# Neighbourhood attention's scores from split operands; the convolution's end and PE's waits rearranged

## The chip, the cores and the metric

One core of one Trainium2 chip. The metric is the device time of one execution in microseconds. The core has the engines PE (matmuls), DVE (elementwise and reductions), ACT (activations, copies), POOL (GpSimd) and SP (here it only issues DMAs). Each works through its own queue in order; semaphores tie the queues together.

## What is computed

A block of 256 rows of width 2048 (feed-forward, attention, feed-forward), then two hybrid layers on it and on a context of 256 rows, all in fp32. What matters here is the mixer of a hybrid layer:

```python
def mix_out(p, na_out, ...):
    ya = multiscale_pool(p[..., OFF_A_V:OFF_A_G], ...) * silu(p[..., OFF_A_G:OFF_B_Q])
    yb = na_out * silu(p[..., OFF_B_G:OFF_C_U])
    yc = conformer_conv(p[..., OFF_C_U:OFF_C_G], ...) * silu(p[..., OFF_C_G:PROJ_WIDTH])
    return concatenate([ya, yb, yc]) @ w_out

# neighbourhood attention, 16 heads of 64 columns: q, k turned by axial_rope,
# scores of local keys (with bias rpb, masked) and of the context's keys, one softmax over both
s_loc = einsum(q * 64**-0.5, k) + bias;  s_ctx = einsum(q * 64**-0.5, kc)
p = softmax(concatenate([s_loc, s_ctx]));  out = p_loc @ v + p_ctx @ vc

def conformer_conv(u, conv_dw, conv_dw_b, ln_g, ln_b, conv_pw, conv_pw_b):
    y = u[..., :512] * sigmoid(u[..., 512:])
    y = depthwise_conv(y, conv_dw, 31 taps) + conv_dw_b
    yn = layer_norm(y) * ln_g + ln_b
    return silu(yn) @ conv_pw + conv_pw_b
```

In the first hybrid layer the context's rows go through all of it too (their queries see the context's keys only); in the second they give keys and values only.

## The kernel before

**The ring.** All weights stream from HBM through one ring: SP loads 512 KB units, ACT copies each 512-column piece to `hi` as fp32r (L392), DVE makes `lo` = raw - hi (L396), and PE takes three single-pass fp32r products for each piece and row tile, in `mm3`: hi by hi (L401), lo by hi (L402), hi by lo (L403). The three together stand in for an fp32 product. Before a projection the activations are turned and split in the same way (`hT`, `uT`).

**A hybrid layer** (`ly` 0 and 1, with `nt` = 4 and 2 row tiles) is: norm and modulation (`z_turn`, `rows_over`, in which PE spreads the row norms with a product of `ones` and `sdg`); five chunks of w_in, ca0 or ca1, with pooling and gated convolution input beside them; the chunks q, k, v, g of w_in, whose results go to `qkvg`, while DVE runs the 31 taps of the convolution (L1578), 128 steps on `cv`, which a memset clears first; then the convolution's end; then the neighbourhood section; then w_out.

**The convolution's end.** DVE adds the bias to `cv` (L1589, semaphore cf_b). PE waits for that, for cpw and cpb (cf_in: two DMAs that SP can issue only when the ring's last piece is used) and for all copies out of the banks, and turns `cv` into four banks (L2128). DVE takes the statistics, ACT the root; then for each tile t: DVE `zb` (L1609), PE turns it (`normed_turn`, L2137), ACT makes `sT` (L960), PE multiplies by cpw in fp32 (`pointwise`, L2147 and L2148), DVE multiplies by the gate (`conv_gate`, L1604). PE's order is turn(t + 1), pointwise(t). ACT makes Silu of the attention's gates behind all this (L967). GpSimd adds the mask to the bias table `ball` in eight instructions, as soon as that table has landed (L2329).

**The neighbourhood section** runs eight pairs of heads, one to a lap (`na_laps`). A unit is one head and one row tile; the two context tiles of `ly` = 0 make one unit of their own. U is 6 or 4 units to the pair. For a pair, DVE turns q and k by the rope into `st` (`rope`, halves 0 and 1, L1629 to L1633), ACT copies the context's part (`stage_ctx`), PE turns all 8 or 6 tiles of `st` into cg[0] and cg[1] (`staged`, L2167), DVE and ACT take them into the one tile `T` (`take_q` L1641, `take_k` L981). For a unit, PE makes the scores in fp32 from 64 rows of T (`na_scores`, L2179: one 128x512 product; L2182: two of 256 columns for the context unit), which stand in the records as two each; DVE adds the bias and takes the maximum (`na_max`, L1655, or L1659 and L1661); ACT the exponentials (`na_exp`, L987 or two of L991); PE turns them (`na_turn`, L2192); ACT copies them to `pt` (`na_pt`, L1000); PE multiplies by the values (`na_values`, L2205, eight records of 64 columns); DVE scales and gates (`na_out`, L1675). Each queue is written out by `step(lap, k, end)`: PE does scores(k + 1), turn(k), values(k - 1); the next pair's rope is at k = 1, `staged` and the takes are at k = U - 2. Nothing of the next pair can be written to T before the last scores from it.

## Time and profile before

| | us |
|---|---|
| runs, median of 3 | 3500.91 (3496.03 to 3502.13) |
| profiled execution, own time | 3507.94 |
| its span, first to last instruction | 3506.0 |
| PE busy | 3376.7 (96%) |
| DVE busy | 2281.8 (65%) |
| ACT busy | 1546.0 (44%) |
| DMA, mean share of 16 engines | 54% |

A busy share is an average over stages. PE's records overlap (a product's record ends when its last column is out, and the next has begun by then), so the pitch from start to start, not the length of a record, says what a product costs PE. "PEclk" is the clock that PE was granted, 1.00 for 2.4 GHz and 0.50 for 1.2 GHz. A window's mean between the two has both in it. Times in rows are us from the start of the span.

### The profile page before, as it was taken

How to read it: one execution, taken by the hardware profiler on the slowest of the kernel's cores; microseconds unless marked ns; L12 is line 12 of the kernel's file. 1: busy time of each engine (PE TensorE's matmuls, PEld its weight loads, DVE VectorE, ACT ScalarE, POOL GpSimd, SP SyncE). 2: the span in 40 equal slices, each digit the busy share in tenths (PEclk: the TensorE clock that was granted, in tenths of full speed). 3: DMA queues.
4: the chain of work that ended last, by engine and by line, in shares of the span. 5: the costliest groups of instructions: out<-in, count | busy, mean ns of one | idle time of the engine just before them, and what ended most of it. 6: DMA issues, size and time to landing. Idle time of an engine off the chain costs nothing.

```text
span 3506.0 us, 40632 instructions
## 1 busy us (share of the span) xinstructions
PE 3376.7 (96%) x15130; PEld 2715.5 (77%) x15130; DVE 2281.8 (65%) x4129; ACT 1546.0 (44%) x2894; POOL 45.0 (1%) x50
## 2 busy tenths in 40 slices
PE   8999999999999999999999999999899989999898
PEld 6788878888887888887887888888567767888566
DVE  6788887777775888887776335555364346646465
ACT  5444444456655444444554222222353344323354
POOL 0000000000000000000000000000100000000100
PEclk9999999999999999999999999999799999999699
DMA  7777777775556777777774323333103245534224
GB/s 266 251 258 259 258 259 250 259 238 168 156 157 210 255 258 255 256 252 261 252 261 156 96 84 96 96 96 98 50 1 120 85 137 157 156 96 130 78 68 161
DMA packets 285002, 613.77 MB, mean 175 GB/s; under 512 B 18882, under 2 KB 21506, under 8 KB 282884
## 3 DMA queue, kind: packets, MB, share of 16 engines
q1 hardware_dynamic: 280804, 596.26, 52.5%
q0 software_dynamic: 2048, 9.37, 0.9%
q10 hardware_dynamic: 1952, 5.54, 0.4%
q8 instruction: 120, 1.97, 0.2%
q14 instruction: 78, 0.64, 0.1%
HBM read 604.80 MB, written 6.29 MB: 174 GB/s over the span
## 4 chain that ended last, share of the span: by engine, by line
PE 76%; DVE 10%; DMA 8%; ACT 4%; issue 2%; ACTq 0%; SPq 0%; DVEq 0%
PE acc L401 23%; PE acc L403 22%; PE acc L402 22%; DMA raw<-ffn_w_gu 7%; DVE lo L396 3%; PE acc L2179 2%; PE acc L2205 2%; ACT hi L392 2%; DVE cgw L1151 1%; DVE mw L1153 1%; PE tp L2192 1%; DMA raw<-ffn_w_down 1%; PE tp L2147 1%; PE tp L1820 0%; DVE tm L1715 0%
## 5 line engine op out<-in xcount | busy, mean ns | idle before, releaser
L392 ACT ACTIVATE hi<-raw 128x512 fp32r<-128x512 f32 x1808 | 1116.0, 630 | 1584.9 <-PE acc L403 1282.6
L396 DVE TENSOR_TENSOR lo<-raw,hi 128x512 fp32r<-128x512 f32 x1808 | 1208.7, 689 | 930.9 <-ACT hi L392 923.0
L401 PE MATMUL acc<-hi,hT_hi 128*128 128x512 f32 x1760 | 703.8, 400 | 30.3 <-DVE hT_lo L1138 15.4
L401 PE MATMUL acc<-hi,h_hi 128*128 128x512 f32 x1696 | 676.0, 399 | 22.6 <-DVE lo L396 17.7
L402 PE MATMUL acc<-hi,hT_lo 128*128 128x512 f32 x1760 | 688.3, 391 | 0.0
L403 PE MATMUL acc<-lo,hT_hi 128*128 128x512 f32 x1760 | 688.3, 391 | 0.0
L403 PE MATMUL acc<-lo,h_hi 128*128 128x512 f32 x1696 | 663.7, 391 | 0.0
L402 PE MATMUL acc<-hi,h_lo 128*128 128x512 f32 x1696 | 663.1, 391 | 0.0
L401 PEld LDWEIGHTS acc<-hi,hT_hi 128*128 128x128 f32 x1760 | 332.2, 189 | 121.6 <-DVE hT_lo L1138 23.6
L401 PEld LDWEIGHTS acc<-hi,h_hi 128*128 128x128 f32 x1696 | 320.1, 189 | 103.2 <-DVE lo L396 31.7
L403 PEld LDWEIGHTS acc<-lo,hT_hi 128*128 128x128 f32 x1760 | 332.1, 189 | 70.7
L402 PEld LDWEIGHTS acc<-hi,hT_lo 128*128 128x128 f32 x1760 | 332.6, 189 | 68.1 <-issue 2.6
L403 PEld LDWEIGHTS acc<-lo,h_hi 128*128 128x128 f32 x1696 | 319.9, 189 | 68.6
L402 PEld LDWEIGHTS acc<-hi,h_lo 128*128 128x128 f32 x1696 | 320.5, 189 | 63.4
L401 PE MATMUL acc<-hi,uT_hi 128*128 128x512 f32 x704 | 276.6, 393 | 4.6 <-DVE uT_lo L1071 3.1
L402 PE MATMUL acc<-hi,uT_lo 128*128 128x512 f32 x704 | 274.6, 390 | 0.0
L403 PE MATMUL acc<-lo,uT_hi 128*128 128x512 f32 x704 | 274.6, 390 | 0.0
L1151 DVE CUSTOM_DVE_ANT_0 cgw<-mw,cb 128x1024 f32<-128x1024 f32 x192 | 235.5, 1227 | 0.0
L1153 DVE CUSTOM_DVE_ANT_0 mw<-mw,cb 128x1024 f32<-128x1024 f32 x192 | 234.5, 1221 | 0.0
L401 PEld LDWEIGHTS acc<-hi,uT_hi 128*128 128x128 f32 x704 | 132.6, 188 | 34.7 <-DVE lo L396 3.8
L1578 DVE SCALAR_TENSOR_TENSOR cv<-yT,dw,cv 128x512 f32<-128x512 f32 (+1 forms) x256 | 156.9, 613 | 0.0
L403 PEld LDWEIGHTS acc<-lo,uT_hi 128*128 128x128 f32 x704 | 132.6, 188 | 27.8
(275 smaller groups left out, 2307.8 us busy)
## 6 DMA issues: line engine op xcount, KB each, us to landing
raw<-ffn_w_gu SPq DMA_DIRECT2D x352, 512.0 KB, 5.6
raw<-w_in SPq DMA_DIRECT2D x280, 512.0 KB, 3.7
mw<-wmt SPq DMA_DIRECT2D x192, 512.0 KB, 5.3
raw<-ffn_w_down SPq DMA_DIRECT2D x176, 512.0 KB, 5.3
raw<-w_out SPq DMA_DIRECT2D x96, 512.0 KB, 4.2
ball<-rpbx SPq DMA_DIRECT2D x8, 768.0 KB, 8.4
x_rest<-x POOLq DMA_DIRECT2D x2, 2048.0 KB, 9.5
x<-x_rest SPq DMA_DIRECT2D x2, 2048.0 KB, 8.0
```

The lines of the kernel that those rows point to most:

```text
L392: act.activation(hi[:, g % RING, :], raw_piece(g), ACT.Copy).then_inc(S["hi_made"], 1)
L396: dve.tensor_tensor(lo[:, g % RING, :], raw_piece(g), hi[:, g % RING, :].bitcast(F32), ALU.subtract).then_inc(S["lo_made"], 1)
L401: pe.matmul(bank, act_hi, hi[:, slot, :], start=start, stop=False)
L402: pe.matmul(bank, act_lo, hi[:, slot, :], start=False, stop=False)
L403: return pe.matmul(bank, act_hi, lo[:, slot, :], start=False, stop=stop)
L1151: dve.tensor_tensor_reduce(cgw[:].rearrange("p a n -> p (a n)"), w, c[:, 0], 1.0, 0.0, ALU.mult, ALU.add, dst[:, 0:1])
L1153: dve.tensor_tensor_reduce(w, w, c[:, 1], 1.0, 0.0, ALU.mult, ALU.add, dst[:, 1:2])\
L1578: dve.scalar_tensor_tensor(out=av, in0=yv, scalar=dw[:, ly, bass.ds(j * 16 + s, 1)], in1=av, op0=ALU.mult, op1=ALU.add).then_inc(S["conv_s ...
L2147: pe.matmul(tp[t % 2][:], sT[:, t % 2, c * P:(c + 1) * P], cpw[:, c, :], start=(c == 0), stop=False)
L2179: ins = pe.matmul(acc[u % 2][:], T[r, t * P:(t + 1) * P], T[r, CH:2 * CH], start=True, stop=True)
L2192: ins = pe.transpose(tp[u % 2][:, j * P:(j + 1) * P], src, ident[:])
L2205: ins = pe.matmul(acc[2 + u % 2][:, k * NA_D:(k + 1) * NA_D], lh, qkvg[:, 2, j if t < 2 else 2 + j, pair_cols(lap, u // U, e * NA_D, NA_D) ...
```

## The change

- **Scores.** T becomes two pairs of tiles, Th and Tl, in fp32r. ACT makes the high parts (`hi_q`, `hi_k`), DVE what is left (`lo_q`, `lo_k`), and a unit's scores are three single-pass products, hh, lh and hl.
- **The lap.** With two pairs of tiles the next pair is staged at k = 1 and taken at k = 1 and 2, and the rope and stage_ctx of the pair after it are at k = U. Two pairs are roped ahead of the first lap.
- **The convolution's end.** The bias goes into `cv` where memset was; L1589 and cf_b go. PE waits for each bank instead of all, and for cf_in only ahead of the first pointwise product. The gates' Silu and the first stage_ctx come before the root on ACT; rope(0, 0) comes between two steps of the convolution's end on DVE, and `staged(0, 0)` before its last pointwise product.
- **Products of constants.** `fill` multiplies `ones` by `dw` into a free bank n times; the products are used nowhere. It stands at five places.

```diff
-        T = at("T", H + 4 * K1, [P, 2 * CH])
+        Th = [at(f"Th{k}", H + (4, 35)[k] * K1, [P, 2 * CH], F32R) for k in range(2)]
+        Tl = [at(f"Tl{k}", H + (31, 23)[k] * K1, [P, 2 * CH], F32R) for k in range(2)]
...
 # ACT, now ahead of the root of the layer norm
+                act.wait_ge(S["acc_taken"], phases[f"mx{ly}"].taken)
+                act.activation(qkvg[:, 3, 0:nt], qkvg[:, 3, 0:nt], ACT.Silu).then_inc(S["gates_made"], 1)
+                stage_ctx(0, 0)
                 act.wait_ge(S["z_made"], (5 if ly else 0) + 1)
                 act.activation(sv[:, 0:nt], sv[:, 0:nt], ACT.Sqrt).then_inc(S["cf_sd"], 1)
...
-                def take_k(lap, n):
-                    act.wait_ge(S["cg_done"], lap * 2 + (cgs + 2 * n + 2))
-                    act.activation(T[:, CH:2 * CH], cg[1][:], ACT.Copy).then_inc(S["cg_taken"], 1)
+                def hi_q(pair):
+                    act.wait_ge(S["cg_done"], cgs + 2 * pair + 1)
+                    act.activation(Th[pair % 2][:, 0:nt * P], cg[0][:, 0:nt * P], ACT.Copy,
+                                   scale=NA_D ** -0.5).then_inc(S["th_made"], 1)
+                def hi_k(pair):
+                    act.wait_ge(S["cg_done"], cgs + 2 * pair + 2)
+                    act.activation(Th[pair % 2][:, CH:2 * CH], cg[1][:], ACT.Copy).then_inc(S["th_made"], 1)
...
                 def step(lap, k, end):
-                    if k == 1 and end > U:
-                        stage_ctx(lap, 1)
+                    if k == U and lap < 6:
+                        stage_ctx(lap, 2)
                     if k + 1 < end:
                         na_exp(lap, k + 1)
-                    if k == U - 2 and end > U:
-                        take_k(lap, 1)
+                    if k == 1 and end > U:
+                        hi_q(lap + 1)
+                    if k == 2 and end > U:
+                        hi_k(lap + 1)
                     if k < end:
                         na_pt(lap, k)
...
 # DVE
-                        dve.memset(cv[:, j - 4], 0.0).then_inc(S["conv_step"], 1)
+                        k = 4 * ly + j - 4
+                        dve.tensor_scalar(cv[:, j - 4], ones[:, 0:1].broadcast_to([P, 2 * L]), cvec[:, k:k + 1], None,
+                                          ALU.mult).then_inc(S["conv_step"], 1)
...
-                dve.wait_ge(S["conv_step"], 132 * (ly + 1))
-                for c in range(4):
-                    av = cv[:, c, 0:nt * P]
-                    dve.tensor_scalar(av, av, cvec[:, 4 * ly + c:4 * ly + c + 1], None, ALU.add).then_inc(S["cf_b"], 1)
...
+                def lo_q(pair, ly=ly, nt=nt):
+                    dve.wait_ge(S["th_made"], 16 * ly + 2 * pair + 1)
+                    dve.scalar_tensor_tensor(out=Tl[pair % 2][:, 0:nt * P], in0=cg[0][:, 0:nt * P], scalar=NA_D ** -0.5,
+                                             in1=Th[pair % 2][:, 0:nt * P].bitcast(F32), op0=ALU.mult,
+                                             op1=ALU.subtract).then_inc(S["cg_taken"], 1)
+                def lo_k(pair, ly=ly):
+                    dve.wait_ge(S["th_made"], 16 * ly + 2 * pair + 2)
+                    dve.tensor_tensor(Tl[pair % 2][:, CH:2 * CH], cg[1][:], Th[pair % 2][:, CH:2 * CH].bitcast(F32),
+                                      ALU.subtract).then_inc(S["cg_taken"], 1)
...
                 def step(lap, k, end):
                     na_sum(lap, k - 1)
-                    if k == 1 and end > U:
-                        rope(lap, 1, 0)
+                    if k == U and lap < 6:
+                        rope(lap, 2, 0)
                     if k + 1 < end:
                         na_max(lap, k + 1)
-                    if k == U - 2 and end > U:
-                        take_q(lap, 1)
+                    if k == 2 and end > U:
+                        lo_q(lap + 1)
                     na_out(lap, k - 1)
-                    if k == 1 and end > U:
-                        rope(lap, 1, 1)
+                    if k == 2 and end > U:
+                        lo_k(lap + 1)
+                    if k == U and lap < 6:
+                        rope(lap, 2, 1)
...
 # DVE: zb, gates and the first ropes (was: all zb and gates, then rope(0, 0), take_q(0))
+                for t in range(nt):
+                    if t >= 2:
+                        dve.wait_ge(S["cz_done"], (4 if ly else 0) + t - 1)
+                    dve.tensor_scalar(zb[:, t % 2], acc[t][:], mv[:, t, 0:1], sv[:, t:t + 1], ALU.subtract,
+                                      ALU.mult).then_inc(S["z_made"], 1)
+                    if t == 1:
+                        dve.wait_ge(S["na_in"], 48 * (ly + 1))
+                        rope(0, 0, 0)
+                        rope(0, 0, 1)
+                    if t >= 1:
+                        conv_gate(t - 1)
+                conv_gate(nt - 1)
+                dve.wait_ge(S["gates_made"], ly + 1)
+                lo_q(0)
+                lo_k(0)
+                rope(0, 1, 0)
+                rope(0, 1, 1)
                 na_max(0, 0)
...
 # PE
+            def fill(bank, n):
+                for _ in range(n):
+                    pe.matmul(bank[:, 0:2 * P], ones[:], dw[:].rearrange("p a n -> p (a n)"), start=True, stop=True)
...
+            fill(acc[3], 4)
             pe.wait_ge(S["const_in"], 16 * 2)
...
             x_turn(phases["n1"], 0, x_in(0))
+            fill(acc[3], 6)
...
             down_proj(phases["d2"], 2 * FC, d2_side)
+            pe.wait_ge(S["mod_done"], 2 * MODS)
+            fill(cg[1], 4)
             pe.wait_ge(S["w_made"], 8)
             z_turn(x1, 0, 3 * CH)
+            fill(cg[1], 2)
             rows_over(0, 0, 4)
+            fill(cg[1], 5)
...
-                pe.wait_ge(S["cf_b"], 4 * (ly + 1))
-                pe.wait_ge(S["cf_in"], 32 * (ly + 1))
-                wait(pe, "acc_taken", phases[f"mx{ly}"].taken)
+                fill(cg[0], 4)
+                pe.wait_ge(S["conv_step"], 132 * (ly + 1))
                 pe.wait_ge(S["yt_taken"], 4 * (ly + 1))
                 for t in range(nt):
+                    pe.wait_ge(S["acc_taken"], phases[f"mx{ly}"].taken - nt + t + 1)
...
-                        ins = pe.matmul(acc[u % 2][:], T[r, t * P:(t + 1) * P], T[r, CH:2 * CH], start=True, stop=True)
+                    qh, ql = (v[(lap + u // U) % 2] for v in (Th, Tl))
+                    for tt in range(1 if t < 2 else 2):
+                        qs = slice((t + tt) * P, (t + tt + 1) * P)
+                        ks = slice(CH, 2 * CH) if t < 2 else slice(CH + L, 2 * CH)
+                        dst = acc[u % 2][:] if t < 2 else acc[u % 2][:, tt * L:(tt + 1) * L]
+                        pe.matmul(dst, qh[r, qs], qh[r, ks], start=True, stop=False)
+                        pe.matmul(dst, ql[r, qs], qh[r, ks], start=False, stop=False)
+                        ins = pe.matmul(dst, qh[r, qs], ql[r, ks], start=False, stop=True)
...
-                    if k == U - 2 and end > U:
+                    if k == 1 and end > U:
                         staged(lap, 1)
...
+                fill(cg[0], 6)
+                normed_turn(0)
+                for t in range(nt):
+                    if t + 1 < nt:
+                        normed_turn(t + 1)
+                    if t == 0:
+                        pe.wait_ge(S["cf_in"], 32 * (ly + 1))
+                    if t == nt - 1:
+                        pe.wait_ge(S["s_made"], (4 if ly else 0) + nt)
+                        staged(0, 0)
+                    pointwise(t)
                 na_scores(0, 0)
                 na_scores(0, 1)
+                pe.wait_ge(S["yc_made"], (4 if ly else 0) + nt)
                 na_turn(0, 0)
...
                     z_turn(x4, 0, 3 * CH)
                     pe.wait_ge(S["gs_taken"], 8)
+                    fill(cg[1], 2)
                     rows_over(1, 0, 2)
+                    fill(cg[1], 7)
```

## Rows read from the trace of the kernel before

**Rows 1.** The page's strip: the clock granted to PE in 40 slices.

```profile
PEclk9999999999999999999999999999799999999699
```

**Rows 2.** A window: PE, PEld, DVE, ACT, POOL busy, PEclk, DMA share, GB/s.

```profile
3318.00:3324.00 6.00, 6.00 (x25) 3.96 (x24) 2.63 (x10) 1.89 (x4) 0.00 (x0) 0.68 0.00 0
```

**Rows 3.** The instructions in order of time, in the ring: start, length, engine, line.

```profile
2440.06 0.39 PE L403 MATMUL acc<-lo,hT_hi 128*128 128x512 f32 x1
2440.29 0.39 PE L401 MATMUL acc<-hi,hT_hi 128*128 128x512 f32 x1
```

**Rows 4.** The same view: a lap of layer 0 at the full clock.

```profile
2535.16 1.09 PE L2167 MATMUL cgw<-ident,st 128*128 128x128 f32 x8
2537.82 1.12 PE L2179 MATMUL acc<-T 64*128 64x512 f32 x2 [0.30 <-ACT T L981]
2540.30 1.12 PE L2179 MATMUL acc<-T 64*128 64x512 f32 x2
2541.35 0.42 PEld L2192 LDWEIGHTS tp<-ident,pr 128*128 128x128 f32 x4 [0.76 <-ACT pr L987]
2542.30 0.72 ACT L987 ACTIVATE pr<-pr,nm 128x512 f32<-128x512 f32 x1 [1.20 <-DVE nm L1655]
2547.04 0.42 PEld L2192 LDWEIGHTS tp<-ident,pr 128*128 128x128 f32 x4 [1.48 <-ACT pr L991]
2552.11 1.09 PE L2167 MATMUL cgw<-ident,st 128*128 128x128 f32 x8
```

**Rows 5.** The same view: two units of layer 0 at half the clock.

```profile
2506.21 2.07 PE L2179 MATMUL acc<-T 64*128 64x512 f32 x2
2510.86 2.07 PE L2179 MATMUL acc<-T 64*128 64x512 f32 x2
```

**Rows 6.** The same view: layer 1, GpSimd beside DVE, first turn, one lap, the end.

```profile
3268.97 14.39 POOL L2329 TENSOR_TENSOR ball<-ball,mask 128x768 f32<-128x768 f32 x8 [7.27 <-DMA ball<-rpbx]
3273.99 0.69 DVE L1604 TENSOR_TENSOR gC<-tp,gC 128x512 f32<-128x512 f32 x1 [8.25 <-PE tp L2148]
3279.93 3.58 DVE L1632 TENSOR_TENSOR rn<-qkvg,ropn 128x128 f32<-128x128 f32 x2
3291.65 0.72 PEld L2192 LDWEIGHTS tp<-ident,pr 128*128 128x128 f32 x4 [1.51 <-ACT pr L987]
3343.55 0.87 PE L2167 MATMUL cgw<-ident,st 128*128 128x128 f32 x6 [0.86 <-DVE st L1633]
3355.11 0.87 PE L2167 MATMUL cgw<-ident,st 128*128 128x128 f32 x6 [0.87 <-DVE st L1633]
3393.00 0.61 PE L2241 MATMUL tp<-ident,ya 128*128 128x128 f32 x4
```

**Rows 7.** The same view: layer 0, the convolution's end, first turn, the section's end.

```profile
2457.85 3.64 PE L2128 MATMUL acc<-ident,cv 128*128 128x128 f32 x16 [5.84 <-DMA cpb<-conv_pw_b]
2463.41 1.53 DVE L1609 TENSOR_SCALAR zb<-acc,mv,sv 128x512 f32<-128x512 f32 x2
2490.27 0.69 DVE L1604 TENSOR_TENSOR gC<-tp,gC 128x512 f32<-128x512 f32 x1 [3.99 <-PE tp L2148]
2494.18 1.94 PE L2167 MATMUL cgw<-ident,st 128*128 128x128 f32 x8 [3.95 <-issue]
2500.51 0.72 PEld L2192 LDWEIGHTS tp<-ident,pr 128*128 128x128 f32 x4 [1.50 <-ACT pr L987]
2640.43 0.92 PEld L2241 LDWEIGHTS tp<-ident,ya 128*128 128x128 f32 x8
```

**Rows 8.** The same view: from the second feed-forward block to ca0.

```profile
1863.70 2.07 PE L1788 MATMUL cgw<-sdg,ones 128*128 128x512 f32 x2 [1.01 <-DVE sdg L1122]
1868.41 0.80 PE L401 MATMUL acc<-hi,hT_hi 128*128 128x512 f32 x1 [2.64 <-DVE hT_lo L1138]
```

**Rows 9.** The same view: the kernel's start.

```profile
11.81 0.77 PE L401 MATMUL acc<-hi,h_hi 128*128 128x512 f32 x1 [4.20 <-DVE h_lo L1091]
17.86 0.39 PE L403 MATMUL acc<-lo,h_hi 128*128 128x512 f32 x1
```

68 lines of the change are left out of this document (19 added, 49 removed).

## The prediction

> **What bounds the kernel now.** I read the page's strip first. PE is busy in nearly every slice, and it runs at the full clock (2.4 GHz) but for two slices with a granted clock of 0.7 and 0.6 [rows 1]. They are the two neighbourhood sections, one for each layer. Inside them it is at half (1.2 GHz) for a good while and then full: a unit takes 4.65 at 2506 and 2.48 at 2538 in layer 0 [rows 4, 5], and in layer 1 the window in which the clock turns, the one from 3318, has 0.68 [rows 2]. Elsewhere PE streams 512-column single-pass products every 0.23 us (0.227 over several) [rows 3], and no edit touches those stretches but for their first microseconds. So the change is worth what it does to (a) the end of the convolution up to the first turn of probabilities, (b) the units of the neighbourhood lap, (c) the clock in both, (d) two short starts.
>
> In a warm lap of layer 0 the chain is PE's: a unit's scores take from 2540.30 to 2541.35 (1.05), then its four turns and eight value products 1.43, and units follow each other in 2.48. A lap of six units and eight staging turns takes 16.95 [rows 4]. 6 x 2.48 + 0.87 of staging is 15.75, so 1.2 are stalls: one is 0.8 long, before the turn at 2547.04, which waits for the exponentials of the context unit, behind half a rope on DVE; the other is 0.36, scores waiting for T. Layer 1 has laps of four units in 11.56 [rows 6]: 9.92 + 0.65, and 1.0 of stalls. At half clock a unit takes 4.65.
>
> **Part by part.**
>
> **The scores.** Two records of 0.427 pitch and about 0.2 behind them, where PE changes from 64 to 128 rows, are the 1.05. Three single-pass products of the ring's pitch are 0.68 [rows 3]; I leave the 0.2 in, as the row count still changes: 0.88, so 0.17 less for each unit, and 2.31 for the unit. For the 256-column products of the context units no row stands; between half the ring's pitch (0.12) and its whole (0.227) six of them and the 0.2 give 0.9 to 1.56, against 1.06 now. I take 0.9, since the turns of 128 columns already follow each other in about 0.11; the upper end would add 0.66 x 16 = 10.6.
>
> The Trainium skill, "TensorE: Matmul & The Clock Gate", section "Measured speedup vs the span model", says that a weight load overlaps running products only when its row group differs. The three products share theirs, so by that rule no load would be hidden. The trace disagrees for 128 rows: loads of the same rows go out while a product runs. It is the second rival below.
>
> **The lap.** Double Th and Tl take the 0.36 for T away. The rope moves to the last step, and there it stands ahead of the maximum of the next lap's unit 1, and its second half ahead of the context unit's. I followed one lap through the three queues, with 2.0 from the start of scores to the start of the exponentials [rows 4] (1.75 with the shorter scores), 0.8 for these and 1.57 for half a rope. The staging turns cover the first half. The context unit's turn then waits 0.5, and its exponentials and hi_q (one ACT pass over 512 columns, by the 0.72 of the exponentials' pass) are both ahead of the copy pt that the next values need: 0.7. So 1.2 stall again, in other places. Lap: 6 x 2.31 + 0.87 + 1.2 = 15.9, 1.0 less. Layer 1: 4 x 2.31 + 0.65 + 0.6 = 10.5, 1.1 less. From the first turn to the end of the section, all at full clock, that is 123.5 in layer 0 and 81.3 in layer 1. The stretch took 139.9 from 2500.51 to 2640.43 [rows 7], and 101.3 from 3291.65 to 3393.0 [rows 6], each with 20 to 30 us of half clock. All warm would be 16.4 and 20.0 less. lo_q and lo_k (by the gate's 0.69 of the same form [rows 7]) and hi_q and hi_k replace takes of the same length, plus one pass each, on engines that are half idle: nothing, but the 0.7 already counted.
>
> **The convolution's end, layer 0.** PE waited 5.84 for cpb, which only the pointwise product needs; the bias adds hid in that. Now PE fills (four products, 1.7) and turns cv from 2453.6 instead of 2457.85 [rows 7]. Turns at full clock and no bias adds give 0.7 more; ACT now has the gates' Silu and a table load ahead of the square root, between nothing and 1.3 back, I take 0.5: zb starts 4.5 before 2463.41. cpb lands at 2457.8 as before, ahead of its new user. The pointwise chain stays; at full clock its first tile is 1.1 shorter, and the staging inside it costs 0.9. So the last gate starts 4.8 earlier, at 2485.5. From there on DVE has gate 0.6, lo_q and lo_k 1.4, both halves of rope(0, 1) 3.1 (gate and two halves lie between 2490.27 and the staging at 2494.18) and then the first maximum, then the exponentials: first turn 6.8 after, 2492.2. It was 2500.51: **8.3 less**. If DVE's queue holds nothing up it is 3 more; if the clock drops in the pauses of the turns, 1 to 2 less.
>
> **The same in layer 1.** The last gate comes near 3272.6 instead of 3278.6. But GpSimd adds the mask to the bias from 3268.97 to 3283.36, in eight instructions of 1.8, and DVE's L1632, with both inputs in SBUF, then took 3.58 for a pair that elsewhere takes 0.62 [rows 6]: each operation waits for the end of one of GpSimd's. rope(0, 1) has eight such operations and now falls into that stretch, ahead of the first maximum. Five of them end with GpSimd's, three take 1.1 more: maximum at 3284.6, first turn at 3286.2 instead of 3291.65: **5.4 less**. The gate, with one input in PSUM, took 0.69 meanwhile, and lo_q and lo_k have that form. The Trainium skill, "SBUF — State Buffer", section "SBUF: two separate sides", calls this an exclusive lock held for a whole instruction, for DVE operations with two SBUF inputs against GpSimd's that read SBUF; the trace agrees.
>
> **The clock.** The fills carry PE from the ring to the turned cv. None stands between the last pointwise product and the first turn of probabilities. In layer 0 that leaves 2 us of nothing, 1.8 of scores, 2.9 of nothing; in layer 1 the second pause is 10 us. Before, it fell in just this place, in both. I expect it to fall in layer 1 surely and in layer 0 likely, and to come back as before, some laps on: in both sections it did in the stretch with the staging turns. One us at half clock costs 0.43 us in this mix (a unit takes 4.3 instead of 2.31, and some stalls hide behind it). I take 18 us after the first turn in layer 0 and 30 in layer 1: 7.7 and 12.8 of the 16.4 and 20.0 are lost. **8.7 and 7.2 less** stay.
>
> **The starts.** Between the second feed-forward block and ca0 PE's 512-column product of the norms takes 2.07 at half clock and the ring starts cold at 1868.41 [rows 8], for about 6 us, as at the kernel's start [rows 9]. With fill(cg[1]) before, between and behind, both run at full clock: 1.0 + 3.0 = **4.0 less** (nothing at least, if DVE's norm chain is next). Each fill fits: 1.7, 0.9 and 2.1 before things that come 2.8, 1.0 and 2.6 later. Before ca1 the same fills buy nothing, as DVE paces those pieces. At the kernel's start the ring is cold from 11.81 to 17.86 [rows 9]; full clock would be worth 2.9 of PE, but DVE and the weight DMA come next: I take **1.3**, from -1 (six cold fills last to 12.7) to 2.9. tensor_scalar for memset on cv costs DVE 0.2 eight times in a stretch that PE bounds: nothing.
>
> **Sum.** 8.3 + 5.4 + 8.7 + 7.2 + 4.0 + 1.3 = 34.9. The profiled execution took 3507.94 (span 3506.0 and 1.9 around it), so 3473; it stands 7.0 above the median 3500.91, of which 34.9 leaves 3466. I say 3467.
>
> **The rivals.**
> - **The low clock stays** through both sections: three passes are less work for the array than two double ones, and the turns and values are short. For: it came back late, in layer 1 some 30 us after the first turn. Against: once back, it stayed to the end of both. Price: 0.43 for each us; all-warm gain is 55.4 in all, so it decides from 55.4 / 0.43 = 130 us of half clock in the mixes. Throughout (215 and 145 us) the kernel takes about 3590: slower. Chance 0.05.
> - **Weight loads of the same 64 rows aren't hidden**: 3 x (0.227 + 0.19) + 0.2 = 1.45 for the scores, 0.57 more than I take, for 80 units: 3466 + 46 = 3512, slower. For: all rows of T are 64 and I have only the ring's of 128. Against: the second load of a score product goes out 0.15 behind the first. Chance 0.05.
> - **Another queue bounds the lap**: with 0.17 gone from PE, the loop of maximum, exponentials, copy and rope sets 2.48 again, or the 256-column products cost their upper end. 13.6 + up to 2 lost: 3480 to 3486. Chance 0.17.
> - **The clock holds** in layer 0 (7.7 more), maybe returns sooner in layer 1: 3447 to 3459. Chance 0.20.
> - The change doesn't do what it says (each gain is DVE's, none PE's): within 7 us. Chance 0.03.
>
> **How the numbers follow.** Forecast 0.50, with its own range 3459 to 3480. The range 3448 to 3491 takes in the clock case and the other queue and leaves out the two slow rivals and the tails. A measurement tells about 0.2% (7 us) from no change. Faster 0.87, the same 0.04, slower 0.09.
>
> **What would show it.** Score products: three at 0.22 to 0.23 pitch, and S to turn 0.88; laps at full clock 15.9 and 10.5. zb of layer 0 comes 10 us earlier than before (4.5 here, 5.3 from the starts), near 2453.6. First turn of layer 1 behind GpSimd's last addition, with rope operations of 1.77. Half clock after the last pointwise products in both. No product at 0.43 pitch around 1870. It is wrong if the lap is still 16.9 warm (queues), or if the granted clock in the two slices is under 0.6.

## The result, and the profile after

The change made the kernel slower. The kernel after takes 3526.01 us (median of 5, 3514.78 to 3527.34), the kernel before 3496.18 (median of 5, 3494.44 to 3502.13): a ratio of 1.0066, with a 95% interval of 1.005 to 1.0081. The profiled execution took 3526.01 with a span of 3524.0, against 3507.94 and 3506.0.

The strip of PE's clock, from the page of the kernel after (40 slices of the span, tenths of the full clock):

```profile
PEclk9999999999999999999999999999999999999569
```

Against [rows 1], layer 0's dip is gone (a slice of 0.9), and layer 1's has grown from one slice of 0.6 to two of 0.5 and 0.6; a clock under 0.6 there was one of the prediction's two signs of being wrong. The next view is of windows of the kernel after: PE, PEld, DVE, ACT, POOL busy, PEclk, DMA share, GB/s. The first two are laps of layer 0, the others stretches of layer 1.

```profile
2544.20:2560.50 16.30, 14.97 (x104) 12.49 (x104) 10.98 (x36) 9.78 (x26) 0.00 (x0) 0.99 0.01 1
2560.50:2578.40 17.90, 16.52 (x105) 14.07 (x105) 11.05 (x37) 9.89 (x26) 0.00 (x0) 0.91 0.01 1
...
3318.00:3331.60 13.60, 12.88 (x47) 10.33 (x47) 6.07 (x20) 4.52 (x12) 0.00 (x0) 0.50 0.00 0
3332.00:3338.00 6.00, 4.48 (x30) 3.45 (x30) 3.14 (x10) 1.81 (x5) 0.00 (x0) 1.00 0.02 4
3339.00:3345.00 6.00, 5.75 (x20) 4.11 (x19) 4.16 (x13) 1.86 (x5) 0.00 (x0) 0.50 0.00 0
3345.00:3383.00 38.00, 35.80 (x132) 28.95 (x130) 14.88 (x50) 12.72 (x30) 0.00 (x0) 0.50 0.00 0
3393.00:3413.00 20.00, 20.00 (x80) 17.06 (x80) 6.13 (x22) 7.83 (x19) 0.00 (x0) 0.50 0.08 16
```

PE is busy 94% of the stretch from 3345 and gets half the clock. In layer 0 the clock drops for 3.4 us in every second lap, and that lap takes 17.9 instead of 16.4. In layer 1 it comes back three times for 3.5 to 6.8 us, falls again each time (3318.0, 3338.5, 3393.1), and is still at half when w_out's ring begins. From the first turn of probabilities to the end of the section layer 1 has 123.9 us of half clock, where it had 30.2 before.

In order of time, the kernel after, a lap of layer 0 at full clock. It answers to [rows 4]:

```profile
2544.16 1.09 PE L2191 MATMUL cgw<-ident,st 128*128 128x128 f32 x8 [1.36 <-DVE st L1625]
...
2546.46 0.50 PE L2208 MATMUL acc<-Th 64*128 64x512 f32 x1
...
2546.80 0.40 PE L2209 MATMUL acc<-Th,Tl 64*128 64x512 f32 x1
...
2547.04 0.39 PE L2210 MATMUL acc<-Tl,Th 64*128 64x512 f32 x1
2547.36 0.42 PEld L2219 LDWEIGHTS tp<-ident,pr 128*128 128x128 f32 x4 [0.37 <-issue]
...
2549.67 0.42 PEld L2219 LDWEIGHTS tp<-ident,pr 128*128 128x128 f32 x4 [0.36 <-issue]
```

Scores to turn is 0.90, turn to turn 2.31: both as forecast. The first row also has a wait that I had not forecast: PE stands idle for 1.36 ahead of the staging turns of each lap, until DVE's rope has written `st`. The three short falls of the clock in layer 0 come near the end of this wait (2526.1, 2560.2, 2594.3). The row at the first of them:

```profile
2526.26 1.97 PE L2191 MATMUL cgw<-ident,st 128*128 128x128 f32 x8 [1.38 <-DVE st L1625]
```

The same view of layer 1, from the end of the convolution to the end of the section; it answers to [rows 6]:

```profile
3251.67 14.79 POOL L2370 TENSOR_TENSOR ball<-ball,mask 128x768 f32<-128x768 f32 x8 [8.51 <-DMA ball<-rpbx]
...
3257.33 3.59 DVE L1624 TENSOR_TENSOR rn<-qkvg,ropn 128x128 f32<-128x128 f32 x2
...
3267.31 0.68 DVE L1653 CUSTOM_DVE_ANT_1 pr<-acc,ball 128x512 f32<-128x512 f32 x1
...
3268.99 1.09 PE L2219 MATMUL tp<-ident,pr 128*128 128x128 f32 x4 [10.86 <-ACT pr L995]
...
3318.47 0.79 PE L2208 MATMUL acc<-Th 64*128 64x512 f32 x1 [1.52 <-DVE Tl L1639]
...
3336.13 0.50 PE L2208 MATMUL acc<-Th 64*128 64x512 f32 x1 [1.52 <-DVE Tl L1639]
...
3364.09 1.54 PE L2191 MATMUL cgw<-ident,st 128*128 128x128 f32 x6 [0.24 <-DVE st L1625]
...
3383.61 1.54 PE L2191 MATMUL cgw<-ident,st 128*128 128x128 f32 x6 [0.24 <-DVE st L1625]
...
3409.93 1.06 PE L2280 MATMUL tp<-ident,ya 128*128 128x128 f32 x4
```

A lap takes 19.52 (3364.09 to 3383.61) where most took 11.56. And there is a second wait that I had not looked for: PE waits for `Tl` ahead of the new pair's first scores in each lap of layer 1, 1.52 at full clock and 0.97 at half, and with or just behind the wait of 1.52 the clock falls (3318.0, 3338.5, 3393.1). What stands behind such a wait, on ACT and DVE, in the kernel after, the last lap but one:

```profile
3388.79 0.72 ACT L995 ACTIVATE pr<-pr,nm 128x512 f32<-128x512 f32 x1 [2.15 <-DVE nm L1653]
...
3389.51 0.58 ACT L989 ACTIVATE Th<-cgw 128x512 fp32r<-128x512 f32 x1
...
3390.12 0.69 DVE L1639 TENSOR_TENSOR Tl<-cgw,Th 128x512 fp32r<-128x512 f32 x1 [0.45 <-ACT Th L989]
...
3390.87 0.50 PE L2208 MATMUL acc<-Th 64*128 64x512 f32 x1 [1.52 <-DVE Tl L1639]
```

`hi_k` and `lo_k` stand at k = 2. A lap of six units has its next scores at k = 5, a lap of four at k = 3: in layer 1 exponentials, `hi_k`, `lo_k` and the scores that need them come one behind the other.

### The profile page after: what moved, and what is told of

Same layout as the page of the kernel before. It is cut to its first block and busy times, and to the rows that moved or that the text cites. A ratio compares the mean times of both kernels' runs of the same rounds, so it can differ in the third digit from the quotient of the medians.

```text
span 3524.0 us, 41047 instructions
## 1 busy us (share of the span) xinstructions
PE 3409.9 (97%) x15326; PEld 2775.8 (79%) x15326; DVE 2295.9 (65%) x4137; ACT 1553.4 (44%) x2910; POOL 45.3 (1%) x50
## 5 line engine op out<-in xcount | busy, mean ns | idle before, releaser
L403 PE MATMUL acc<-hi,h_hi 128*128 128x512 f32 x1696 | 673.4, 397 | 20.6 <-DVE lo L398 17.2
L403 PEld LDWEIGHTS acc<-hi,hT_hi 128*128 128x128 f32 x1760 | 331.7, 188 | 117.0 <-DVE hT_lo L1149 19.5
```

What stands on the lines that cost most here:

```text
L403: pe.matmul(bank, act_hi, hi[:, slot, :], start=start, stop=False)
```

## The experiments

All ratios are to the kernel before, run on the same chip. "L1" is layer 1 from its first turn to the end of the section, of it "half" at half clock, both in us; these two and the falls are from the profiled execution.

| run | ratio [95%] | L1 | half | falls in layer 0's laps |
|---|---|---|---|---|
| before | 1 | 101.3 | 30.2 | 0 |
| after | 1.0066 [1.005, 1.0081] | 140.9 | 123.9 | 3 |
| after_fp32_scores | 0.9947 [0.9932, 0.9962] | 104.0 | 25.5 | 0 |
| before_split_scores | 1.0156 [1.0135, 1.0176] | 122.7 | 88.6 | half clock for 133 us |
| after_no_constants | 1.0103 [1.0088, 1.0118] | 145.3 | 135.1 | 3 |
| after_fourth_product | 1.0117 [1.0095, 1.0138] | 134.4 | 86.6 | 0 |
| after_lap_constants | 1.0259 [1.0225, 1.0294] | 143.4 | 25.6 | 1 |
| fp32_scores_takes_early | 0.9941 [0.9918, 0.9964] | 98.8 | 25.5 | 0 |
| fp32_scores_gap_filled | 0.9946 [0.9919, 0.9974] | 87.9 | 0 | 1 |
| fp32_scores_no_constants | 0.9963 [0.9947, 0.9979] | 96.5 | 5.6 | 0 |
| split_gap_filled | 1.0051 [1.0032, 1.0069] | 141.7 | 120.9 | 3 |
| split_gap_and_light_lap_products | 1.0077 [1.005, 1.0105] | 143.0 | 93.5 | 0 |
| fp32_scores_gap_filled_4_10 | 0.9912 [0.9891, 0.9934] | 88.2 | 0 | 0 |
| after_turns_twice | 1.0100 [1.0069, 1.013] | 113.2 | 19.5 | 1 |
| after_five_products | 1.0174 [1.0146, 1.0202] | 153.4 | 117.7 | 0 |
| after_one_fp32_product | 1.0066 [1.0038, 1.0094] | 147.1 | 123.2 | 0 |
| after_takes_early | 0.9962 [0.9947, 0.9977] | 112.3 | 67.1 | 2 |
| one_fp32_product_takes_early | 0.9928 [0.9903, 0.9953] | 98.7 | 25.3 | 0 |
| split_gap_filled_takes_early | 0.9947 [0.9921, 0.9972] | 99.9 | 30.7 | 3 |

The profiled execution is not always a typical one. In before_split_scores it was the slowest of four (3585.78, median 3559.14); in after_turns_twice (3517.66, median 3532.01), after_fourth_product (3531.33, median 3545.56) and after_five_products (3547.52, median 3561.67) the fastest. Where a main reading rests on the half clock of one execution, the mean clocks of the others are given too.

### Are the split scores the cause?

after_fp32_scores, beside the tiles and takes:

```diff
-                        pe.matmul(dst, qh[r, qs], qh[r, ks], start=True, stop=False)
-                        pe.matmul(dst, ql[r, qs], qh[r, ks], start=False, stop=False)
-                        ins = pe.matmul(dst, qh[r, qs], ql[r, ks], start=False, stop=True)
+                        ins = pe.matmul(dst, T_[r, qs], T_[r, ks], start=True, stop=True)
```

> The changed kernel with the scores back in fp32 (one product of full precision from each of two tiles T, which alternate as Th and Tl did); lap order, convolution's end and products of constants stay. Theory A, the split scores give the array so little work per microsecond that its clock falls inside the laps: no fall inside the warm laps of layer 0 any more, layer 1 at half clock for about 40 us from its first turn and not 124, so its section falls from 140.9 to about 97, at 0.17 more for each of 80 units (+14): median near 3490. Rival B, it is the 10.9 us in which PE waits ahead of layer 1's first turn, and the reordered convolution's end that made them, whatever the scores are: half clock throughout layer 1 here too, near 3535.

Measured: 0.9947. Layer 1 had 25.5 us of half clock behind a wait of 9.42 ahead of its first turn (10.86 in the kernel after), and then the full clock to the end, with laps of 12.37. So the split scores and what goes with them cost 1.2%, some 42 us, and the rest of the change gains 0.5%. What goes with them is work on ACT and DVE (`hi_q` and `lo_k` are gone here too), and with it PE's waits: 0.80 ahead of the new pair's first scores in layer 1 instead of 1.52, and 1.05 for the rope in layer 0 instead of 1.36. Rival B is out. Windows of after_fp32_scores, columns as above:

```profile
3270.00:3295.00 25.00, 24.89 (x78) 16.59 (x79) 8.19 (x28) 8.17 (x19) 0.00 (x0) 0.50 0.01 1
...
3344.00:3374.00 30.00, 27.23 (x169) 19.40 (x168) 14.00 (x52) 14.84 (x34) 0.00 (x0) 1.00 0.00 1
```

before_split_scores puts the same three products into the kernel before, with single tiles Th and Tl taken where T was:

```diff
-                        ins = pe.matmul(acc[u % 2][:], T[r, t * P:(t + 1) * P], T[r, CH:2 * CH], start=True, stop=True)
+                        pe.matmul(dst, Th[r, qs], Th[r, ks], start=True, stop=False)
+                        pe.matmul(dst, Tl[r, qs], Th[r, ks], start=False, stop=False)
+                        ins = pe.matmul(dst, Th[r, qs], Tl[r, ks], start=False, stop=True)
```

> The kernel before with only its scores split in three single-pass products (Th and Tl single tiles, ACT's copies and DVE's subtractions at the place of the old takes). Theory A: the falls appear here too, a few short ones in layer 0's laps and most of layer 1's section at half clock: 30 to 40 us lost there, near 3525. Rival B: nothing of the gap is in it, so the clock comes back as before and 80 units are 0.17 shorter, less a few tenths for each lap's extra subtractions: near 3487.

Measured: 1.0156, worse than either theory gave. In the profiled execution layer 0 stayed at half clock for 133 us from 2496, and from 2504 on no row of PE has a wait in front of it (window of before_split_scores):

```profile
2503.00:2600.00 97.00, 96.64 (x372) 81.34 (x372) 40.31 (x132) 35.89 (x96) 0.00 (x0) 0.50 0.00 1
```

The kernel before got its clock back 27 us after 2492.4 in the same laps with fp32 scores, and there PE was busy all the time too. With 96.64 of 97 us busy no wait is to blame: for the way back from half clock it is what the work is made of. The other three executions had mean clocks of 0.958 to 0.965, against 0.980 or 0.981 in the kernel before, so they lost clock too, though less. In layer 1 of this run the falls at 3386.9 and 3417.7 stand behind waits of 1.19 and 1.17 for the rope, where the kernel before has 0.86 or 0.87.

### Does more work on PE bring the clock back?

> The changed kernel with the product hi by hi of each unit's scores issued twice (the second overwrites the first), so the array has a third more work in the scores, at the same waits. Theory A: the laps hold the full clock or get it back early; PE pays 0.23 for each of 80 units (+18), layer 1's section gives back 30 to 40: near 3505. Rival B: the clock doesn't change and the products cost 0.23 to 0.43 each: near 3550.

```diff
+                        pe.matmul(dst, qh[r, qs], qh[r, ks], start=True, stop=True)
                         pe.matmul(dst, qh[r, qs], qh[r, ks], start=True, stop=False)
```

Layer 0: no fall in its laps (17.2 each, 0.84 more), as theory A had it; but the wait for the rope is down from 1.36 to 0.90 too. Layer 1 alternated, 10.2 us at half clock in each lap of 17.1, so the time was missed: the median, 3545.56, is where rival B had it.

> The changed kernel, scores split, with products of constants inside the laps: eight of 256 columns ahead of the staging turns, where PE waits 1.36 for the rope, and three ahead of the turns of units from k = 3 on, where it waits 0.36. Theory A (too little work for the array per microsecond): no fall in layer 0's laps, full clock back in layer 1 within 40 us of the first turn; laps stay 16.4 there and come to about 11 in layer 1: near 3490. Rival D, it isn't the amount of work but the kind of product (64 rows, or the change of rows from one product to the next) that keeps the clock low: as the changed kernel, 3530 or more.

```diff
                     if k == 1 and end > U:
+                        fill(cg[1], 8)
                         staged(lap, 1)
+                    if k >= 3 and end > U:
+                        fill(cg[1], 3)
```

The clock did much of what theory A says: the mean of layer 1 is 0.91, and that of a long stretch of layer 0 1.00, with one fall in its laps where none was expected. The products also fill the wait for the rope, so the run does not separate amount of work from wait. The time missed by far: 1.0259. I had let three products of `fill` fit into 0.36, but a product is fp32, two records of 0.21 (the prediction had four of them right, at 1.7), and what I took for a wait of PE ahead of a turn is none (below). Laps of layer 0 took 24.38, 8.0 more. Rows of after_lap_constants, in order of time:

```profile
2551.72 1.04 PE L2191 MATMUL cgw<-ident,st 128*128 128x128 f32 x8
...
2561.54 1.56 PE L1795 MATMUL cgw<-dw,ones 128*128 128x256 f32 x6
...
2576.09 1.04 PE L2191 MATMUL cgw<-ident,st 128*128 128x128 f32 x8
```

> split_gap_filled with single-pass products of 256 columns (0.11 each) inside the laps, eight ahead of the staging turns (0.9 of a wait of 1.36) and three ahead of each turn from k = 3 on (0.33 of 0.36): array work only where PE waits. The products of after_lap_constants were fp32, 0.43 each, and made laps of layer 0 8.0 longer, with no fall in them. Theory A: most of the falls go; laps of layer 0 16.4 to 16.7, layer 1 11 to 12, near 3480, if this much more work is enough; if it isn't, layer 1 alternates and the time is 3500 to 3520. If the amount of array work had nothing to do with the clock: as split_gap_filled.

```diff
-                        fill(cg[1], 8)
+                        light(Th[lap % 2], 8)
...
+                pe.matmul(cg[1][:, 0:2 * P], tile[:, 0:P], tile[:, CH:CH + 2 * P], start=True, stop=True)
```

Single-pass products at the same places, on top of split_gap_filled (below). Layer 0 held its clock, but its laps came to 18.30, not 16.4 to 16.7: the 0.36 ahead of each turn stands on the row of the weight loads (PEld) alone, and PE's row has no wait there, so the three products cost their whole price (turn to turn 2.72). Layer 1 went on alternating, each fall at or behind a wait of 1.52 for `Tl`. Nothing was gained.

> The changed kernel with each of the four turns of a unit's probabilities issued twice (same result), so PE has 0.44 more work in each unit at full clock, all of it turns, where after_fourth_product had 0.23 more, all of it product, and no fall inside layer 0's laps. If any work of PE counts for the clock alike: no fall in layer 0's laps here either, layer 1 at half clock for at most the 87 us of after_fourth_product. If turns count little or nothing and it is products that hold the clock: three or more falls inside layer 0's laps, or layer 0 at half clock for most of the section, and layer 1 at half clock for over 120 us, since the products are spread thinner. Time 3560 in the first case, 3580 to 3650 in the second.

```diff
+                        pe.transpose(tp[u % 2][:, j * P:(j + 1) * P], src, ident[:])
                         ins = pe.transpose(tp[u % 2][:, j * P:(j + 1) * P], src, ident[:])
```

The first case, but for one fall in layer 0's laps (at 2609.3, behind a wait of 1.11 for the rope), and faster than expected: 80 units with 0.44 of useless turns in each, 35 us, and the ratio is 1.0100 against the 1.0066 of the kernel after. From 3316 on layer 1 was at full clock with laps of 13.84. That is the fastest of four executions, with a mean clock of 0.988; the others had 0.980 to 0.985, still above the 0.971 to 0.976 of the kernel after.

> The changed kernel with the product hi by hi of each unit issued three times, so 0.46 more of single-pass product in each unit, where after_turns_twice had 0.44 more of fp32 turns. If time spent streaming is what counts: layer 1 as there, at half clock for under 40 us after its first turn, then full with laps near 13.8, median near 3535. If single-pass products count less than fp32 ones for their time: layer 1 goes on alternating, 60 us or more at half clock, median 3555 or more.

```diff
+                        pe.matmul(dst, qh[r, qs], qh[r, ks], start=True, stop=True)
+                        pe.matmul(dst, qh[r, qs], qh[r, ks], start=True, stop=True)
                         pe.matmul(dst, qh[r, qs], qh[r, ks], start=True, stop=False)
```

Single-pass products for as much time as the doubled turns, and layer 1 was at half clock for 117.7 us. That was the expectation's second case, and it looked like a matter of the form of the products. But the two differ in something else. One wait of each, in layer 1 at full clock, first after_turns_twice, then after_five_products:

```profile
3333.68 0.50 PE L2208 MATMUL acc<-Th 64*128 64x512 f32 x1 [1.09 <-DVE Tl L1639]
```

```profile
3313.15 0.49 PE L2208 MATMUL acc<-Th 64*128 64x512 f32 x1 [1.52 <-DVE Tl L1639]
```

The second stands 1.9 us ahead of a fall at 3315.0. after_fourth_product, split_gap_filled and its variant with light products have the 1.52 too. The wait of 1.08 in after_turns_twice is not without falls either: behind the one at 3300.51 the clock fell once, at 3302.2.

### The wait for the low half

> The changed kernel with the three single-pass products replaced by one fp32 product of Th by Th (the low parts are still made but not used: the scores leave them out). Only PE's products differ from the changed kernel, 0.17 more for each unit at full clock. If the cause is in the products alone, as all of theory A says: layer 1 at half clock for 25 to 45 us after its first turn and then full, no fall inside layer 0's laps, median 3480 to 3495, as after_fp32_scores. If ACT's or DVE's extra work on the halves had a share in it: between 3495 and 3525.

```diff
+                        ins = pe.matmul(dst, qh[r, qs].bitcast(F32), qh[r, ks].bitcast(F32), start=True, stop=True)
```

Measured: 1.0066 [1.0038, 1.0094], the ratio of the kernel after, and the expectation of theory A for layer 1 and for the time is refuted. Layer 0 had no fall in its laps (its wait for the rope is 1.05), layer 1 fell and stayed down for 109 us behind a wait for a half that the product doesn't even read. after_one_fp32_product, a row and a window:

```profile
3311.30 1.22 PE L2208 MATMUL acc<-Th 64*128 64x512 f32 x1 [1.52 <-DVE Tl L1639]
```

```profile
3311.00:3415.00 104.00, 99.79 (x313) 67.21 (x313) 36.33 (x122) 31.14 (x74) 0.00 (x0) 0.50 0.00 1
```

So in layer 1 the wait for the halves in each lap has to go. That takes one digit in three places:

```diff
-                    if k == 2 and end > U:
+                    if k == 1 and end > U:
                         hi_k(lap + 1)
...
-                    if k == 2 and end > U:
+                    if k == 1 and end > U:
                         lo_q(lap + 1)
...
-                    if k == 2 and end > U:
+                    if k == 1 and end > U:
                         lo_k(lap + 1)
```

(`hi_q` stood there already.)

> The changed kernel with all four takes (hi_q, hi_k, lo_q, lo_k) of the next pair at k = 1, so the first scores of a pair find their halves made. PE's wait of 1.52 in each lap of layer 1 goes. Theory F (the wait in each lap keeps layer 1 cold): full clock back within 45 us of the first turn and laps near 10.8, median 3475 to 3490. Theory A (the split products are too little even without the wait): 80 us or more at half clock in layer 1, median 3510 or more. Layer 0, which has no such wait, keeps its three short falls in both.

> after_one_fp32_product (low halves made, not used) with the same takes at k = 1. In both theories layer 1 gets its clock back, as in after_fp32_scores: 25 to 45 us at half clock, laps of 11.5 at full clock, median near 3485. If it stays at half clock, neither the wait nor the products are the cause, and ACT's and DVE's load is.

> split_gap_filled with the takes at k = 1. Theory F: no half clock in layer 1 at all, laps 10.8, median near 3468, the best of the split kernels. Theory A: layer 1 starts warm and falls, as split_gap_filled did at 3278: near 3515.

Measured: 0.9962, 0.9928 and 0.9947. With three lines the change is faster than the kernel before, 1.04% or 36 us faster than as it was made. The four kernels that differ in the two things alone:

| L1 (half) | takes at k = 2 | takes at k = 1 |
|---|---|---|
| three single-pass products | 140.9 (123.9) | 112.3 (67.1) |
| one fp32 product | 147.1 (123.2) | 98.7 (25.3) |

The mean clocks of all executions say the same as the profiled ones: 0.971 to 0.976 in the kernel after, 0.971 to 0.980 with one fp32 product, 0.980 to 0.983 with early takes, 0.985 to 0.992 with both.

With the takes at k = 1 the fp32 product gets the clock back in 25 us and keeps it. The split products get it back and lose it again for 20.5 us in every second lap. So the wait for the halves decides most. The rest is not shown to be the thinner work, because another wait is left: PE still stands idle ahead of the staging turns until the rope is done. It is longer with the split products, which leave the rope less time to hide in. The falls of after_takes_early in layer 1 (3284.3, 3315.1, 3345.8) all stand 0.6 to 0.9 behind the start of these turns, after waits of 1.19, 1.18 and 1.18. Rows of after_takes_early, then of one_fp32_product_takes_early:

```profile
3344.94 0.33 PE L2191 MATMUL cgw<-ident,st 128*128 128x128 f32 x1 [1.18 <-DVE st L1625]
```

```profile
3320.06 0.87 PE L2191 MATMUL cgw<-ident,st 128*128 128x128 f32 x6 [0.86 <-DVE st L1625]
```

Windows of after_takes_early, then of one_fp32_product_takes_early:

```profile
3304.00:3314.50 10.50, 9.32 (x58) 7.32 (x58) 6.95 (x24) 4.78 (x11) 0.00 (x0) 0.96 0.00 0
3316.00:3335.00 19.00, 18.75 (x71) 15.22 (x70) 8.44 (x27) 7.38 (x18) 0.00 (x0) 0.50 0.01 1
```

```profile
3298.00:3371.00 73.00, 68.38 (x404) 47.21 (x402) 45.86 (x154) 39.28 (x93) 0.00 (x0) 1.00 0.00 1
```

Theory F was right in direction and too sure: 67 us of half clock stayed where it said under 45, and the median, 3493.11, is above its 3490. Layer 0 kept two falls, near the end of its own wait for the rope (1.37). In split_gap_filled_takes_early it expected no half clock in layer 1 and 3468; there were 30.7 us and 3483.88, with falls at 3294.4, 3318.3 and 3331.9, again at or behind waits of 1.18 for the rope. That run had laps of 11.17 at full clock; with one fp32 product it is 11.50. Four units are 0.68 shorter, and the wait for the rope takes 0.32 of it back. The 0.33 a lap that is left, 5 us over 16 laps, is all that the split is worth with the rope where it is, and its falls cost more.

### The gap ahead of the first turn, the takes with fp32 scores, the constants

> after_fp32_scores with both takes of the next pair at k = 1 (T is double, nothing forbids it). There the lap of layer 1 was 12.37 against 11.56 before, with a wait of 0.80 ahead of the first scores from the new T, taken at k = 2 behind an exponential. If that wait is the lap's loss, layer 1's lap is 11.5 and layer 0's stays 16.9: 6 less, a ratio near 0.993. If the loss only moves to the next copy pt: no change.

The edit is that of after_takes_early, for `lo_q` and `hi_k`, which here fill T. The lap of layer 1 came to 11.50 from 12.37, as expected. The ratio, 0.9941 against 0.9947, can't tell the 6 us: one kernel's executions differ by more.

> fp32_scores_takes_early with rope(0, 1) behind the first two maxima on DVE and ten products of constants ahead of the first turn of probabilities, in both layers. In after_fp32_scores PE waited 10 us there in layer 1 and then had 25.5 us of half clock. If rope(0, 1) behind GpSimd's additions is what the first turn waits for, it comes 8 us sooner, but the staging turns of the next pair wait instead, so 2 to 5 are left. If the gap is what makes the clock fall, less of half clock: up to 8 more. Together 3 to 12 below fp32_scores_takes_early.

```diff
-                rope(0, 1, 0)
-                rope(0, 1, 1)
                 na_max(0, 0)
                 na_max(0, 1)
+                rope(0, 1, 0)
+                rope(0, 1, 1)
...
                 pe.wait_ge(S["yc_made"], (4 if ly else 0) + nt)
+                fill(cg[1], 10)
                 na_turn(0, 0)
```

In the profiled execution layer 1 had no half clock left after its first turn and took 87.9. In layer 0 ten products were too many. Seven executions lay between 3472.29 (mean clock 0.993) and 3502.51: the median, 3485.34, is no better than without.

> fp32_scores_gap_filled with 4 instead of 10 products of constants ahead of layer 0's first turn, where ten took 6.97 us at half clock and the exponentials had been done at 2484.2. First turn of layer 0 4 to 5 sooner, nothing else: 3 to 5 below fp32_scores_gap_filled where the clock does the same, ratio near 0.9930.

```diff
-                fill(cg[1], 10)
+                fill(cg[1], 4 if nt == 4 else 10)
```

Measured: 0.9912, better than expected, 3472.65, the best of all. Its strip and layer 1 from the first turn on:

```profile
PEclk9999999999999999999999999999999999999999
```

```profile
3268.50:3356.70 88.20, 82.40 (x487) 56.82 (x486) 52.35 (x183) 45.31 (x105) 0.11 (x1) 1.00 0.00 1
```

> The changed kernel (split scores) with rope(0, 1) behind the first two maxima and products of constants ahead of the first turn of probabilities, 4 in layer 0 and 10 in layer 1. In fp32_scores_gap_filled this took layer 1's half clock after the first turn from 25.5 us to 0. Theory A (split laps give the array too little work at any time): layer 1 begins warm and falls again within a lap or two, 90 us or more at half clock, median 3515 to 3530. Rival E (a fall at the start is what the split laps can't get out of, warm laps would hold): full clock through layer 1, laps of about 10.9, near 3475.

The same edit on the kernel after, with split scores: layer 1 began warm and fell all the same: for 3.4 us at 3271.2, behind a wait of 2.06 for the rope, and for 13.7 us at 3278.0, with a wait of 1.52 for `Tl`. The time, 1.0051, is theory A's. The gap sets when the clock falls first, not whether it stays. Since the wait for `Tl` was still in it, the run does not tell whether split laps would hold without one.

> The changed kernel without any product of constants. Both theories of the laps expect layer 1 unchanged, at half clock for some 124 us from its first turn. By my sum of the starts (1.3 and 4.0) and of the convolution's end it is 5 to 8 slower than the changed kernel: about 3532. Rival C, the constants' power or timing is what upsets the clock later (the new fall at 519, the falls inside laps): near 3490, and no fall at 519.

> after_fp32_scores without any product of constants: what the constants are worth when the laps hold their clock. By my sum 5.3 at the two starts and 1 to 2 at the convolution's end, so 6 slower than after_fp32_scores: ratio near 0.9965. The changed kernel lost 13 without them by the two ratios; if that was the lottery of layer 1's clock, 6 stays here; if the constants are worth 13 by themselves, ratio near 0.9985.

```diff
-                for _ in range(n):
+                for _ in range(0):
                     pe.matmul(bank[:, 0:2 * P], ones[:], dw[:].rearrange("p a n -> p (a n)"), start=True, stop=True)
```

The constants are worth 0.16% with fp32 scores (0.9963 to 0.9947, 5.6 us, intervals that overlap) and 0.37% with split ones (13 us, where I expected 5 to 8). The first is near the 6 that I expected, but the noise is as large. Rival C is out: without the constants layer 0's laps keep their three falls and layer 1 has 135.1 us of half clock. The fall at 519 is absent in both profiles without constants, but so it is in five with them.

## Why the prediction was wrong

**The sum.** From the same products of the ring in both traces, and the landmarks:

| term | forecast, less | measured, less |
|---|---|---|
| the starts | 5.3 | 2.8 |
| layer 0 until the first turn | 8.3 | 8.5 |
| layer 0's mix | 8.7 | 6.7 |
| between the layers | 0 | 0.5 |
| layer 1 until the first turn | 5.4 | 4.2 |
| layer 1's mix | 7.2 | **-39.6** |
| w_out's first pieces | 0 | -1.1 |
| sum | 34.9 | -18.0 |

**The step that failed** is layer 1's lap. I followed a lap of layer 0 through the three queues and wrote "Layer 1: 4 x 2.31 + 0.65 + 0.6 = 10.5" behind it. In layer 1 U is 4, and k = 2 is one step ahead of the new pair's scores, not three. Following that lap gives max, exponentials, `hi_k`, `lo_k`, scores in a row, and PE's wait of 1.52. The wait for T, which I had as gone ("take the 0.36 for T away"; the rows of before have 0.30), had grown. By itself it is 7 x 1.5 = 11, one for each pair staged inside the section; through the clock the term came out 47 worse than forecast.

**The second failure** is a sentence of the clock: "to come back as before, some laps on", and against the first rival "once back, it stayed". That was a statement on laps with 2.48 a unit and waits of at most 0.87, and I carried it over to laps that the change made thinner and gave longer waits. The split laps lose the clock again once they are warm, in layer 0 every 34.1 us and for 3.4 us.

**The third failure** is "The staging turns cover the first half" of the rope. They did not: in layer 0 PE waits 1.36 for it ahead of them, and this is the lap's one stall, where I had two others of 0.5 and 0.7. That the sum of stalls, 1.2, came near is luck.

**The first rival** had the low clock at a chance of 0.05. Its reason ("three passes are less work for the array") is borne out for the way back by before_split_scores, but in the kernel after the wait for `Tl` had the larger part. Half clock after the first turns was 16.3 + 123.9 = 140 us, beyond its 130, and the kernel was slower. By its price of 0.43 that is 60 us against a gain of 55.4, so 5 slower; of the other 13 of the 18 measured, 9 are in the two mixes beside this price and 2.5 in the starts. (Its "about 3590" for half clock throughout should have been 3600 by the same sum: 360 us for 204.8, less 55.4.) It needed no stay through both sections: layer 1 alone was enough. That the order of DVE's and ACT's queues could set off the clock, I had in no case. The third rival had the queues in it, and the rope's wait is one of its kind, but priced only by its own length.

**What was right.** Scores to turn 0.90 for 0.88, units 2.31 for 2.31. Weight loads of the same 64 rows are hidden: the second rival is out, as products follow each other in 0.23 to 0.24. The rule in the Trainium skill that it was measured by ("TensorE: Matmul & The Clock Gate", section "The mechanism", not the section after it, which I had named) says that a weight load overlaps running products only where the row group differs; the trace does not agree with it. A lap of layer 0 took 16.36 for 15.9 where the clock was full (0.6 less than before, not 1.0). Layer 1's first turn came behind GpSimd's last addition, with rope operations of 1.6 to 1.9; the first maximum stood 0.85 behind the last (3266.46 to 3267.31), where I had 1.2. The end of the convolution, [rows 7], in the kernel after:

```profile
2450.78 1.91 PE L2161 MATMUL acc<-ident,cv 128*128 128x128 f32 x16
...
2455.97 1.53 DVE L1700 TENSOR_SCALAR zb<-acc,mv,sv 128x512 f32<-128x512 f32 x2
...
2489.26 1.09 PE L2219 MATMUL tp<-ident,pr 128*128 128x128 f32 x4 [1.98 <-ACT pr L995]
```

zb came 7.4 sooner, not 10; 2.8 of it was brought along, so the convolution's own part was 4.6 for 4.5.

**The starts** were mis-sized. The kernel's start brought 2.5 by 17.5 us and 4.2 by 300, not 1.3. At the turn from the second block to ca0 the kernel after went from 1.2 ahead at 1850 to 4.9 ahead at 1874.6, but waits for `hT_lo` took 2.1 back by 1892: 1.6 stayed, not 4.0. The norms' product was at full clock, as forecast, and none at 0.43 followed ([rows 8]):

```profile
1862.55 1.13 PE L1813 MATMUL cgw<-sdg,ones 128*128 128x512 f32 x2 [0.93 <-DVE sdg L1133]
...
1866.31 0.50 PE L403 MATMUL acc<-hi,hT_hi 128*128 128x512 f32 x1 [0.48 <-DVE hT_lo L1149]
```

Between 300 and 590 us 5.8 were lost, in a stretch that no edit touches, 4.3 of it while the clock was down at 519.0:

```profile
519.00:525.80 6.80, 5.61 (x13) 4.45 (x14) 3.03 (x5) 1.99 (x5) 0.00 (x0) 0.50 0.51 158
```

Eleven of the 19 profiles have it between 517 and 523, also that of before_split_scores, which is the kernel before up to there; the profile of before does not. It is chance, of the size of a term of the sum. Another 2.1 came back between 590 and 1200, where the kernel before had 6.8 us of half clock at 1116.9 and the kernel after 3.4, and 0.7 until 1850: 4.2 - 5.8 + 2.1 + 0.7 + 1.6 = 2.8.

**What stays open.** Whether thinner products make a warm clock fall by themselves, or only through the waits that they lengthen. Every run that shortened a unit also lengthened PE's wait for the rope: with one fp32 product (0.85 of product in each unit) it is 1.05 in layer 0 and 0.86 in layer 1, with three single-pass products (0.68) 1.36 and 1.18, with four (0.91) 0.90 in layer 0. The falls inside warm laps, in all profiles, stand in a wait of PE or up to 2.7 us behind it. Most of these waits are of 1.16 to 2.06, a few of 0.64 to 1.11, and many waits of 1.36 have no fall behind them, so no limit can be read from this. Two runs bear on it, and neither was made: after_takes_early with the rope one step earlier, and the four-product kernel with early takes.

## What to carry to other kernels

A loop that runs with two lengths has to be followed in both: a step that is three ahead of its user in the long one may be one ahead in the short one. Where the array's work is being made thinner, the clock that a profile of before shows is no evidence for after, and a wait of 1.5 us in a lap cost three times itself here (11 us of waiting, 36 us of kernel). Look first for the wait that stands just ahead of each fall of the clock: here, three lines that move the takes by one step turned 0.7% slower into 0.4% faster. Then look again: the wait for the rope stood behind the first one, and it was left in.

## What the runs showed of the hardware

- The clock fell in laps of the kernel after in which PE was busy 14.97 of 16.30 us, with a longest wait of 1.38, and in layer 1 behind waits of 1.52. It stayed at half for 109 us with PE busy 99.79 of 104 (after_one_fp32_product). The Trainium skill, "TensorE: Matmul & The Clock Gate", "HAM oscillation — how this bites in real kernels", puts such swings down to a wait of PE for a DMA in each turn of a loop, of some 3 to 5 us there. The trace agrees that a wait in each turn goes with the swings, but the waits here are shorter and for DVE, and before_split_scores stayed at half clock with no wait at all.
- The same page of the Trainium skill, "Part 4: PE-mode transpose", has it that turns don't count as busy PE for the clock in the same way. 35 us of added turns cost 12 here (1.0066 to 1.0100) and layer 1 got its clock back. They also made the wait for `Tl` shorter, 1.09 instead of 1.52, so no run here separates the two.
- Idle time on PEld's row ahead of a turn, 0.36, was not idle time of PE: products put there cost their whole length.
- Executions of one kernel differ by the granted clock: 3472.29 at 0.993 and 3498.84 at 0.983 for fp32_scores_gap_filled.
